# Second layer of a two-layer trunk: the four groups of heads are taken in the order second, first, fourth, third

## The chip, the core and the metric

The kernel runs on one core of a Trainium2 chip. The metric is device time in microseconds (us) of one execution. The engines are TensorE (PE in the profile), VectorE (DVE), ScalarE (ACT), GpSimd (POOL) and SyncE (SP); SP, ACT and POOL each also issue DMA transfers, which all run on the core's 16 DMA engines.

## The reference

The model has two layers over x (1, 512, 2048), float32. The change touches the second one only: an attention layer with forget gates, 16 heads of 128 columns.

```python
h = rms_norm(x, norm_g)
proj = h @ w_in                       # w_in: (2048, 4*2048 + 16), columns [q | k | v | z | forget logits]
q, k, v, z, f_logit = jnp.split(proj, [2048, 4096, 6144, 8192], axis=-1)
q, k = rms_norm(q per head), rms_norm(k per head)
cum = jnp.cumsum(log_sigmoid(f_logit + f_bias), axis=1)          # one row for each head
for each head, block of 128 queries:
    logits = q . k * 128**-0.5 + cum[query] - cum[key];  causal mask;  p = softmax(logits);  out = p @ v
y = out * silu(z)
x = x + y @ w_out                     # w_out: (2048, 2048), 128 rows for each head
```

## The kernel before, in words

Every large product is computed in split precision: an operand is divided into a high and a low part, and three matmuls replace one. For the input projections of both layers a one-level fast scheme (seven block products for eight) is used as well. It needs sums of weight blocks, which VectorE computes, and one sum per step is stored to a scratch tensor (`t2_dram`, printed as `t_rows`) and read back later.

The input projection of the second layer is made in eight *units*, here called units 0 to 7 (`u - UB` in the code). A unit makes 512 columns of q and 512 of k ("qk"), or 512 of v and 512 of z ("vz"), for all 512 positions. Its list of kinds is `KIND`, and `GROUP` says which group of four heads each unit serves: units 0 and 1 serve the first group taken, units 2 and 3 the second, 4 and 5 the third, 6 and 7 the fourth.

A unit has two phases of eight steps. In each step SP loads 128 rows of the weight (or twice 128 in the first phase, 1 MB in all), into one of three buffers `raw`. Each row of such a load is made of two separate pieces of 512 floats (2048 bytes): for "qk" one of q's columns and one of k's. In the second phase SP also reads back the 256 KB sum. The row pitch of the weight is 8208 floats (32,832 bytes), and a group's pieces begin at `c` = 512 columns times the group's number, in each of the four parts q, k, v, z.

Then DVE forms sums in place (L1624, L1626) and the sum to be stored (L1633), ACT makes the high part (`u_hi`, L714), DVE the low part (`u_lo`, L1639), and PE multiplies (L1192 to L1194): 24 matmuls in a step of the first phase, 18 in one of the second; in unit 0 it is the other way round, and its first-phase loads are 768 KB. SP issues the load of step g only when the low part of step g - 3 is made (`lo1_ready`), so the loads run three steps ahead of L1639.

Other work stands between the steps at fixed places. After a "qk" unit that is followed by a "vz" unit, the heads' q and k are normalized and turned (L1403) and stored. Finished v and z are stored too. Unit 2 also makes the forget gates (L1429 to L1431), for all 16 heads at once, and stores their cumulative rows. In the second half of unit 7 POOL and SP load what attention wants first (`qkT`, `vz`, `accb`), and PE begins with the first head. After unit 7 comes the tail: attention of one pair of heads beside the output projection of the pair before, with rows of `w_out` loaded by `load2`.

The order of all this is written out by hand, engine by engine. Scratch tensors hold heads by their position in the order (`qkT_dram`, `vz_dram`); `cum_dram` holds them by their true number.

Of the kernel before, what the change touches and what calls it, by code (L numbers as in the profile page):

```python
# [31 lines left out]
P = 128  # L32
# [3 lines left out]
def build_trunk(nc, x, a_norm_g, a_w_in, a_v_norm_g, a_w_s, a_b_s, a_w_out,  # L36
                b_norm_g, b_w_in, b_f_bias, b_q_norm_g, b_k_norm_g, b_w_out, out):
    SEQ, D = x.shape[1], x.shape[2]
# [6 lines left out]
    HD = b_q_norm_g.shape[1]  # L45
    FB = 512
# [17 lines left out]
    UB = NU  # L64
    KIND = ["qk", "vz", "qk", "vz", "qk", "vz", "vz", "qk"]
    GROUP = [0, 0, 1, 1, 2, 2, 3, 3]
    NB_U = len(KIND)
    NUT = UB + NB_U
    HG = 4
# [17 lines left out]
    cum_dram = nc.dram_tensor("cum_rows", [H, SEQ], F32).ap()  # L87
# [8 lines left out]
    with ExitStack() as ctx:  # L96
        base = (nc.sbuf_base + 31) // 32 * 32

        def at(name, offset, shape, dt=F32):
            return nc.alloc_sbuf_tensor_at(name, shape, dt, offset=base + offset)  # L100
# [60 lines left out]
        cum_row = at("cum_row", 196608, [P, 2, SEQ])  # L161
# [217 lines left out]
        def products_of(u):  # L379

            own = u >= UB and KIND[u - UB] == "vz"
            return [(e1v if own else e1, c11_ready, 0, 1), (cA, c21_ready, 2, 1),
                    (eU, c12_ready, 0, 0), (e57v if own else e57, c22_ready, 2, 0)]
# [3 lines left out]
        def turns_before(u):  # L387

            return 4 * sum(KIND[b] == "vz" and KIND[b - 1] == "qk" for b in range(1, u - UB))

        def stores_before(u):

            return 4 * sum(KIND[b - 1] == "vz" for b in range(1, u - UB))
# [10 lines left out]
        def before(h):  # L404

            return h - 2 if h >= 3 else h - 1 if h == 1 else None

        def side_of(h):
            return 1 if h % 2 or h == 0 else 0

# [10 lines left out]
        def _(sp):  # L421
# [6 lines left out]
            def weights(u, row):  # L428
                if u < VU:
                    return a_v[row:row + P, u, :, :]  # L430
                if u < NU:
                    return a_uz[row:row + P, :, (u - VU) * FB:(u - VU + 1) * FB]
                c = GROUP[u - UB] * FB
                return (b_qk if KIND[u - UB] == "qk" else b_vz)[row:row + P, :, c:c + FB]

            def load_step(u, ph, k):
                g = step_of(u, ph, k)
                slot, loaded = raw_of(g), raw_wait(g)[0]
                if g >= STEPS + 3:
                    sp.wait_ge(lo1_ready, g - 2)  # L440
                elif g >= STEPS:
                    f = g - STEPS
                    sp.wait_ge(x2_stored[f], 16)
                    sp.wait_ge(x_turned, KP + 2 * f + 2)
                    sp.wait_ge(sqb_ready, NT * (f + 1))
                elif g >= 4:
                    sp.wait_ge(lo1_ready, g - 3)
                k1, k2 = weights(u, 2 * k * P), weights(u, (2 * k + 1) * P)
                if ph == 0:
                    sp.dma_start(slot[:, 1:3, :], k1).then_inc(loaded, 16)  # L450
                    if first(u):
                        sp.dma_start(slot[:, 0, :], k2[:, 0, :]).then_inc(loaded, 16)
                    else:
                        sp.dma_start(slot[:, 0:4:3, :], k2).then_inc(loaded, 16)
                else:
                    q = u * KP + k
                    sp.dma_start(slot[:, 0:4:3, :], k2).then_inc(loaded, 16)
                    sp.wait_ge(t2_stored[q % 2], (q // 2 + 1) * 16)
                    sp.dma_start(slot[:, 2, :], t2_dram[k, :, :]).then_inc(loaded, 16)
# [21 lines left out]

            def load2(i):
                p, f, k = i // (2 * NF), i // 2 % NF, i % 2
                row = (2 * p + k) * HD
                if i >= R:
                    sp.wait_ge(lo_ready, B0 + i - R + 1)
                sp.dma_start(w2_raw[:, i % R, :], b_out[row:row + HD, f * FB:(f + 1) * FB])\
                    .then_inc(w_loaded[i % R], 16)
# [22 lines left out]
            for i in range(R, B0):  # L511
                f, k = i // KY, i % KY
# [3 lines left out]
                if f == 0 and 12 <= k < 24:  # L516
                    if k == 12:
                        sp.wait_ge(lo1_ready, STEPS)
                    t, c = (k - 12) % NT, (k - 12) // NT
# [7 lines left out]
            for u in range(UB, NUT):  # L527
                for ph in range(2):
                    for k in range(KP):
                        if step_of(u, ph, k) >= STEPS + 3:  # L530
                            load_step(u, ph, k)
                        if u == NUT - 1 and ph == 1 and k >= 6:
                            for e in range(2):
                                f = 2 * (k - 6) + e
                                sp.wait_ge(step_done, step_of(u, 1, 3 * (k - 6) + 3))
                                sp.dma_start(accb[f][:, :, :], x2_dram[f, :, :, :]).then_inc(accb_loaded[f], 16)
            sp.wait_ge(lo1_ready, STEPS + NB_U * 2 * KP - 2)
            for i in range(2 * NF * NP):
                load2(i)
# [9 lines left out]
        def _(pool):  # L549
# [81 lines left out]
            def store_products(u):  # L631
                g, n = GROUP[u - UB], stores_before(u + 1) // 2
                bufs = products_of(u)
                for i, (buf, _, t0, _) in enumerate((bufs[2], bufs[3])):
                    pool.wait_ge(v_b, n + i + 1)
                    pool.dma_start(vz_dram[0, g, :, t0:t0 + 2, :], buf[:, :, :]).then_inc(vz_stored, 16)
                for i, (buf, _, t0, _) in enumerate((bufs[0], bufs[1])):
                    pool.wait_ge(z_b, n + i + 1)
                    pool.dma_start(vz_dram[1, g, :, t0:t0 + 2, :], buf[:, :, :]).then_inc(vz_stored, 16)

            for u in range(UB + 1, NUT):
# [3 lines left out]
                elif KIND[b] == "vz":  # L645
                    qk_power(turns_before(u) // 4)
                    for r in range(HG):
                        h = turns_before(u) + r
# [5 lines left out]
                    pool.dma_start(cum_dram, cum_T).then_inc(cum_stored, 16)  # L654

            def load_cum(h):
                pool.dma_start(cum_row[:, h % 2, :], cum_dram[h:h + 1, :].broadcast_to([P, SEQ]))\
                    .then_inc(cum_loaded[h % 2], 16)

            def load_qkT(h):  # L660
# [10 lines left out]
            for s in range(2):  # L671
                pool.wait_ge(qkT_stored[s], 16 * (H - HG) // 2)
            load_cum(0)
            load_cum(1)
            pool.wait_ge(step_done, step_of(NUT - 1, 1, 0))
            load_qkT(0)
# [5 lines left out]
            for h in range(H):  # L682
                if h == 3:
                    qk_power(NP // 2 - 1)
                if h + 2 < H:
                    pool.wait_ge(last_logits, h + 1)
                    load_cum(h + 2)
                if h + HG < H - HG:
                    pool.wait_ge(last_scores, h + 1)
                    load_qkT(h + HG)  # L690
                if h % 2 and h // 2 + 2 < NP:
                    pool.wait_ge(yb_ready, h + 1)
                    load_vz(h // 2 + 2)
# [3 lines left out]
        def _(act):  # L697
# [359 lines left out]
            def exps(h):  # L1057
                s = side_of(h)
                for n, i in enumerate(Q_ROWS[0:3]):
                    p = probs[:, s, row_at[i]:row_at[i] + (i + 1) * P]  # L1060
                    act.wait_ge(logits, 3 * h + n + 1)
                    act.activation(p, p, ACT.Exp, scale=-1.0, bias=nmin[:, s, i:i + 1],
                                   accum_out=rsum[:, s, i:i + 1]).then_inc(probs_ready, 1)

            def last_exp(h):
                s = side_of(h)
                p = probs[:, s, row_at[1]:row_at[1] + 2 * P]
                act.wait_ge(last_logits, h + 1)
                act.activation(p, p, ACT.Exp, scale=-1.0, bias=nmin[:, s, 1:2],
                               accum_out=rsum[:, s, 1:2]).then_inc(last_probs, 1)  # L1070

            def probs_turned(h):
                one, two = bank_of(h)
                act.wait_ge(probsT_psum, h + 1)
                for b, bank in enumerate((one, two)):
                    ins = act.activation(probs_T[:, side_of(h), b * 4 * P:(b + 1) * 4 * P], bank, ACT.Copy)
                ins.then_inc(probsT_ready, 1)
# [1108 lines left out]
```

## Time and profile before

| | us |
|---|---|
| median of 3 runs | 2398.81 (2394.89 to 2402.56) |
| profiled execution, its own time | 2398.87 |
| its span in the trace | 2397.0 |
| PE busy | 2290.7 |
| DVE busy | 1616.3 |
| ACT busy | 1065.4 |

The second layer's projection lies between about 1385 and 2100 us of the span. An engine's busy time is the sum over its instructions; what lies between the instructions is idle time, which the view of waits assigns to the engine or the DMA that ended it. The time that the DMA engines took for a queue's packets is given as a share of 16 engines over the stretch that was asked for.

### The profile page before, as it was taken

Reading aid. Unit: us, or ns where it says so; the run is one execution under the profiler, and the core shown is the slowest. Engines: PE = TensorE matmul, PEld = TensorE weight load, DVE = VectorE, ACT = ScalarE, POOL = GpSimd, SP = SyncE. Lnnn points to the kernel's source line nnn. Section 1 sums busy time; section 2 is a strip of 40 time slices with the busy share of each in tenths; the row PEclk is TensorE's granted clock in tenths of the full one; section 3 lists DMA queues with packets and bytes.
Section 4 is the critical chain, followed back from the end, with each engine's and each line's share of the span. In section 5 each row is a group of like instructions: output and inputs, shape, how many; then the busy total and the mean of one; then the engine's idle time right before and its main releaser. Section 6 shows DMA issues by size and latency. Waiting matters only on the chain.

```text
span 2397.0 us, 26493 instructions
## 1 busy us (share of the span) xinstructions
PE 2290.7 (96%) x10413; PEld 1864.1 (78%) x10413; DVE 1616.3 (67%) x1676; ACT 1065.4 (44%) x1319; POOL 134.1 (6%) x185
## 2 busy tenths in 40 slices
PE   5999999999999999999999989999989999989999
PEld 4777787788888878878888877777767777778887
DVE  6787778777877877753222477776766777566665
ACT  6555445454544544552222544343443344344332
POOL 0011011000000000000000000100100000102000
PEclk9999999999999999999999999999999999999999
DMA  6577787776776767765344568885698897845333
GB/s 207 171 248 248 239 260 247 226 236 220 236 227 219 235 218 239 232 226 164 97 115 115 122 160 165 197 271 161 197 226 197 188 279 231 293 137 163 101 96 116
DMA packets 230252, 474.86 MB, mean 198 GB/s; under 512 B 19600, under 2 KB 23744, under 8 KB 229104
## 3 DMA queue, kind: packets, MB, share of 16 engines
q1 hardware_dynamic: 188416, 363.91, 54.2%
q0 software_dynamic: 18576, 67.28, 8.0%
q10 hardware_dynamic: 23136, 41.98, 4.7%
q8 instruction: 82, 1.34, 0.2%
q14 instruction: 42, 0.34, 0.0%
HBM read 391.28 MB, written 81.82 MB: 197 GB/s over the span
## 4 chain that ended last, share of the span: by engine, by line
PE 72%; DVE 11%; DMA 10%; ACT 3%; issue 2%; SPq 0%; POOL 0%; ACTq 0%; DVEq 0%
PE ps L1192 15%; PE ps L1194 15%; PE ps L1193 15%; DVE u_lo L1639 5%; PE ps L1349 4%; PE ps L1351 4%; PE ps L1350 4%; DMA raw<-in_b_w_in_dram 3%; DMA t_rows<-t 3%; DMA raw<-t_rows 3%; PE ps L1572 2%; PE ps L1574 2%; PE ps L1573 2%; DVE raw L1624 2%; ACT u_hi L714 2%
## 5 line engine op out<-in xcount | busy, mean ns | idle before, releaser
L714 ACT ACTIVATE u_hi<-raw 128x1536 fp32r<-128x1536 f32 (+1 forms) x320 | 544.7, 1702 | 822.7 <-PE ps L1194 788.1
L1639 DVE TENSOR_TENSOR u_lo<-raw,u_hi 128x1536 fp32r<-128x1536 f32 (+1 forms) x320 | 646.9, 2022 | 234.7 <-ACT u_hi L714 234.4
L1192 PE MATMUL ps<-u_hi,x1h 128*128 128x512 f32 x1280 | 515.9, 403 | 69.2 <-DVE u_lo L1639 58.7
L1193 PE MATMUL ps<-u_lo,x1h 128*128 128x512 f32 x1280 | 505.2, 395 | 0.0
L1194 PE MATMUL ps<-u_hi,x1l 128*128 128x512 f32 x1280 | 504.4, 394 | 0.0
L1192 PE MATMUL ps<-u_hi,x2h 128*128 128x512 f32 x960 | 381.0, 397 | 5.9 <-DVE u_lo L1639 5.8
L1194 PE MATMUL ps<-u_hi,x2l 128*128 128x512 f32 x960 | 375.1, 391 | 0.0
L1193 PE MATMUL ps<-u_lo,x2h 128*128 128x512 f32 x960 | 374.9, 391 | 0.0
L1192 PEld LDWEIGHTS ps<-u_hi,x1h 128*128 128x128 f32 x1280 | 243.8, 190 | 153.2 <-DVE u_lo L1639 85.4
L1194 PEld LDWEIGHTS ps<-u_hi,x1l 128*128 128x128 f32 x1280 | 244.1, 191 | 53.0
L1193 PEld LDWEIGHTS ps<-u_lo,x1h 128*128 128x128 f32 x1280 | 244.2, 191 | 48.2
L1624 DVE TENSOR_TENSOR raw<-raw 128x1024 f32<-128x1024 f32 x160 | 194.9, 1218 | 65.1 <-DMA raw<-in_b_w_in_dram 65.0
L1835 DVE TENSOR_TENSOR w_lo<-w_raw,w_hi 128x512 fp32r<-128x512 f32 x128 | 88.2, 691 | 210.3 <-ACT w_hi L922 210.3
L1192 PEld LDWEIGHTS ps<-u_hi,x2h 128*128 128x128 f32 x960 | 181.0, 189 | 45.1 <-DVE u_lo L1639 8.3
L1194 PEld LDWEIGHTS ps<-u_hi,x2l 128*128 128x128 f32 x960 | 180.9, 188 | 38.1
L1193 PEld LDWEIGHTS ps<-u_lo,x2h 128*128 128x128 f32 x960 | 181.2, 189 | 36.6
L1349 PE MATMUL ps<-w_hi,yhl 128*128 128x512 f32 x448 | 175.5, 392 | 0.0
L1351 PE MATMUL ps<-w_hi,yhl 128*128 128x512 f32 x448 | 174.4, 389 | 0.0
L1350 PE MATMUL ps<-w_lo,yhl 128*128 128x512 f32 x448 | 174.3, 389 | 0.0
L922 ACT ACTIVATE w_hi<-w_raw 128x512 fp32r<-128x512 f32 x128 | 80.4, 630 | 208.1 <-PE ps L1351 206.1
L1626 DVE TENSOR_TENSOR raw<-raw 128x512 f32<-128x512 f32 x160 | 111.5, 697 | 51.8 <-DMA raw<-t_rows 51.7
L1633 DVE TENSOR_TENSOR t<-raw 128x512 f32<-128x512 f32 x160 | 109.7, 686 | 47.8 <-DMA t_rows<-t 47.2
(232 smaller groups left out, 2418.5 us busy)
## 6 DMA issues: line engine op xcount, KB each, us to landing
raw<-in_a_w_in_dram SPq DMA_DIRECT2D x280, 512.0 KB, 4.4
raw<-in_b_w_in_dram SPq DMA_DIRECT2D x184, 512.0 KB, 5.5
t_rows<-t ACTq DMA_DIRECT2D x160, 256.0 KB, 4.9
raw<-t_rows SPq DMA_DIRECT2D x160, 256.0 KB, 5.1
w_raw<-in_a_w_out_dram SPq DMA_DIRECT2D x128, 256.0 KB, 2.9
w_raw<-in_b_w_out_dram SPq DMA_DIRECT2D x64, 256.0 KB, 2.7
vz<-vz_rows POOLq DMA_DIRECT2D x16, 512.0 KB, 5.4
t<-yT_rows SPq DMA_DIRECT2D x28, 256.0 KB, 3.8
```

What stands on the lines that cost most here:

```text
L714: act.activation(u_hi[:, u_of(g), 0:n, :], raw_of(g)[:, 0:n, :], ACT.Copy).then_inc(hi1_ready, 1)
L1192: pe.matmul(dst[:, t, :], a, u_hi[:, s, pos, :], start=first, stop=False, skip_group_check=more)
L1193: pe.matmul(dst[:, t, :], a, u_lo[:, s, pos, :], start=False, stop=False, skip_group_check=more)
L1194: mm = pe.matmul(dst[:, t, :], b, u_hi[:, s, pos, :], start=False, stop=last, skip_group_check=more)
L1349: pe.matmul(ps[S][:, t, :], a, w_hi[:, s, :], start=start, stop=False)
L1350: pe.matmul(ps[S][:, t, :], a, w_lo[:, s, :], start=False, stop=False)
L1351: mm = pe.matmul(ps[S][:, t, :], b, w_hi[:, s, :], start=False, stop=stop)
L1624: dve.tensor_tensor(m[:, 0:2, :], m[:, 0:2, :], m[:, 1:3, :], ALU.add).then_inc(t_ready, 1)
L1626: dve.tensor_tensor(m[:, 1, :], m[:, 3, :], m[:, 2, :], ALU.add).then_inc(t_ready, 1)
L1633: dve.tensor_tensor(t2[:, q % 2, :], raw_of(g)[:, 0, :], raw_of(g)[:, 2, :], ALU.add)\
L1639: dve.tensor_tensor(u_lo[:, u_of(g), 0:n, :], raw_of(g)[:, 0:n, :], u_hi[:, u_of(g), 0:n, :].bitcast(F32), ALU.subtract).then_inc(lo1_read ...
L1835: dve.tensor_tensor(w_lo[:, i % R, :], w_raw[:, i % R, :], w_hi[:, i % R, :].bitcast(F32), ALU.subtract).then_inc(lo_ready, 1)
```

## The change

A list `GROUP_COLS = [1, 0, 3, 2]` maps the position in the order to the true group of heads. It enters at three places: the columns of `w_in` that a unit loads, the rows of `w_out` that a pair of heads loads, and the row of `cum_dram` that a head loads. The scratch tensors stay indexed by position. The number, order, shapes and waits of the instructions are the same on all engines; only the addresses in HBM of these three kinds of loads differ.

```diff
     GROUP = [0, 0, 1, 1, 2, 2, 3, 3]
+    GROUP_COLS = [1, 0, 3, 2]
...
+        def head_of(h):
+
+            return GROUP_COLS[h // HG] * HG + h % HG
+
...
-                c = GROUP[u - UB] * FB
+                c = GROUP_COLS[GROUP[u - UB]] * FB
                 return (b_qk if KIND[u - UB] == "qk" else b_vz)[row:row + P, :, c:c + FB]
...
-                row = (2 * p + k) * HD
+                row = head_of(2 * p + k) * HD
...
-                pool.dma_start(cum_row[:, h % 2, :], cum_dram[h:h + 1, :].broadcast_to([P, SEQ]))\
+                pool.dma_start(cum_row[:, h % 2, :], cum_dram[head_of(h):head_of(h) + 1, :].broadcast_to([P, SEQ]))\
```

## Rows read from the trace of the kernel before

**Rows 1.** The page, part 1: busy time, share of the span, instructions.

```profile
PE 2290.7 (96%) x10413; PEld 1864.1 (78%) x10413; DVE 1616.3 (67%) x1676; ACT 1065.4 (44%) x1319; POOL 134.1 (6%) x185
```

**Rows 2.** The line L450: duration ns min/median/max, first and last start.

```profile
L450 SPq DMA_DIRECT2D raw<-in_b_w_in_dram x64: 367/368/1372, 1350.6 to 2039.4; - x64
```

**Rows 3.** Timeline of SP's queue where units 2, 4, 6 begin loading.

```profile
1553.64 0.37 SPq L450 DMA_DIRECT2D raw<-in_b_w_in_dram  x1
...
1734.68 0.37 SPq L450 DMA_DIRECT2D raw<-in_b_w_in_dram  x1
...
1919.36 0.37 SPq L450 DMA_DIRECT2D raw<-in_b_w_in_dram  x1
```

**Rows 4.** DMA queues, 1350 to 1551.9 us: packets, MB, share of 16 engines.

```profile
q1 hardware_dynamic: 15079, 28.59, 69.8%
```

**Rows 5.** DMA queues, 1551.9 to 1732.9 us.

```profile
q1 hardware_dynamic: 15469, 29.59, 57.1%
```

**Rows 6.** DMA queues, 1732.9 to 1917.6 us.

```profile
q1 hardware_dynamic: 15351, 29.35, 80.2%
```

**Rows 7.** DMA queues, 1917.6 to 2088.8 us.

```profile
q1 hardware_dynamic: 15504, 31.07, 62.9%
```

**Rows 8.** The tile raw, from 1380 us on: duration min/median/max, first and last start.

```profile
L1639 DVE TENSOR_TENSOR u_lo<-raw,u_hi x128: 1747/2016/2342, 1384.6 to 2099.9; 128x1536 fp32r<-128x1536 f32 x64, 128x2048 fp32r<-128x2048 f32 x64
```

**Rows 9.** Windows, one for each unit's loads (units 0 to 7).

```profile
core 0: us, PE busy (x) PEld busy (x) DVE busy (x) ACT busy (x) POOL busy (x), PEclk, DMA share, GB/s
1384.60:1460.80 76.20, 69.91 (x296) 55.93 (x296) 57.03 (x55) 36.25 (x40) 2.02 (x2) 0.96 0.74 170
1460.80:1551.90 91.10, 84.53 (x365) 68.03 (x364) 70.19 (x63) 36.64 (x29) 5.43 (x1) 0.98 0.88 181
1551.90:1636.60 84.70, 81.76 (x376) 65.96 (x375) 60.30 (x50) 39.79 (x37) 5.50 (x9) 1.00 0.85 254
1636.60:1732.90 96.30, 92.31 (x455) 73.84 (x453) 69.69 (x65) 39.59 (x34) 6.88 (x2) 1.00 0.59 173
1732.90:1827.20 94.30, 82.92 (x366) 65.65 (x365) 59.51 (x48) 40.93 (x36) 4.33 (x8) 1.00 0.94 222
1827.20:1917.60 90.40, 81.83 (x343) 65.03 (x342) 66.58 (x61) 35.65 (x28) 5.46 (x1) 0.96 0.91 187
1917.60:2000.20 82.60, 80.74 (x364) 65.73 (x363) 59.31 (x49) 39.17 (x35) 4.32 (x8) 1.00 0.85 255
2000.20:2088.80 88.60, 82.31 (x354) 65.30 (x353) 60.80 (x57) 37.47 (x36) 9.45 (x16) 0.98 0.88 286
```

**Rows 10.** Waits, 1732.9 to 1827.2 us (unit 4): us in total, times, longest.

```profile
DVE raw L1624 <- DMA raw<-in_b_w_in_dram: 21.1, 8, 4.6
PE ps L1192 <- DVE u_lo L1639: 11.0, 8, 2.9
```

**Rows 11.** Waits, 1917.6 to 2000.2 us (unit 6).

```profile
DVE raw L1624 <- DMA raw<-in_b_w_in_dram: 7.3, 4, 3.5
PE ps L1192 <- DVE u_lo L1639: 1.6, 2, 0.9
```

**Rows 12.** Waits, 1384.6 to 1460.8 us (unit 0).

```profile
PE ps L1192 <- DVE u_lo L1639: 6.3, 4, 3.0
```

**Rows 13.** Waits, 1460.8 to 1551.9 us (unit 1).

```profile
PE ps L1192 <- DVE u_lo L1639: 6.1, 3, 3.0
```

**Rows 14.** Waits, 1827.2 to 1917.6 us (unit 5).

```profile
PE ps L1192 <- DVE u_lo L1639: 8.1, 4, 3.6
```

**Rows 15.** Windows, the first-phase part of units 2, 4, 6; columns as in rows 9.

```profile
1551.90:1597.90 46.00, 43.73 (x201) 35.05 (x200) 33.29 (x27) 24.69 (x25) 3.78 (x7) 1.00 0.89 282
...
1732.90:1788.00 55.10, 45.97 (x207) 36.01 (x205) 33.48 (x26) 26.11 (x26) 3.80 (x7) 1.00 1.00 230
...
1917.60:1963.30 45.70, 43.84 (x202) 35.23 (x201) 33.46 (x28) 24.45 (x25) 3.78 (x7) 1.00 0.91 277
```

**Rows 16.** DMA queues and issues, 2000.2 to 2088.8 us (unit 7); issues end in us to landing.

```profile
q0 software_dynamic: 1888, 6.82, 20.2%
...
vz<-vz_rows POOLq DMA_DIRECT2D x4, 512.0 KB, 9.4
```

**Rows 17.** Window, the tail; columns as in rows 9.

```profile
2088.80:2397.00 308.20, 297.61 (x1585) 242.68 (x1583) 193.46 (x381) 115.60 (x267) 25.33 (x33) 0.99 0.38 125
```

## The prediction

> **What bounds the kernel now.** I read the page first. PE is busy 96% of the span [rows 1], so the end is set by PE and by whatever makes it wait. The change alters only HBM addresses, so the one thing that can move is how long some loads take. I therefore looked for places where PE waits behind loads, and whether loads of different groups take different times.
>
> The first load of the second layer's projection is issued at 1350.6 us [rows 2]. The loads of the second, third and fourth group begin at 1553.64, 1734.68 and 1919.36 [rows 3]. I cut the trace close to these places and asked each stretch for SP's queue (q1). Its engine time per packet is share x 16 x stretch / packets:
> - group 0: 0.698 x 16 x 201.9 / 15079 = 149.5 ns [rows 4]
> - group 1: 0.571 x 16 x 181.0 / 15469 = 106.9 ns [rows 5]
> - group 2: 0.802 x 16 x 184.7 / 15351 = 154.4 ns [rows 6]
> - group 3: 0.629 x 16 x 171.2 / 15504 = 111.1 ns [rows 7]
>
> That is the reading on which everything rests. Packet counts and bytes are nearly equal (28.6 to 31.1 MB), the kinds of unit are the same, yet the columns of groups 0 and 2 take 40% more engine time than those of groups 1 and 3, and it switches twice back and forth where the group switches. I call them slow and fast groups. Why the address does this, no row says.
>
> Then by unit. The 128 instructions of L1639 [rows 8] are the steps in order. Loads run three steps ahead, so I cut unit n's stretch from its step -3 to its step 13 [rows 9]; unit 0 starts at step 0. Units 4 and 6 are the clean pair: both follow a "vz" unit, with the same stores and the same extra work of DVE and PE. Unit 4 (slow) takes 94.3 us at a DMA share of 0.94, unit 6 (fast) 82.6 at 0.85: 11.7 us apart. The engines' time is 0.94 x 94.3 = 88.6 against 0.85 x 82.6 = 70.2 us, 18.4 us more for slow columns. In unit 4 DVE waits 21.1 us for the weights and PE 11.0 us for DVE [rows 10]; in unit 6 it is 7.3 and 1.6 [rows 11]. The difference is nearly all in the first phase, which asks 1 MB of each step: 55.1 us in unit 4 (DMA share 1.00), 46.0 and 45.7 in units 2 and 6 [rows 15].
>
> **The change part by part.** The columns of w_in: today positions 0 to 3 in the order (units 0-1, 2-3, 4-5, 6-7) are slow, fast, slow, fast. Afterwards they are fast, slow, fast, slow. The slow traffic is not less; it stands beside other work. So units 0, 1, 4, 5 gain, and units 2, 3, 6, 7 lose.
>
> Gains:
> - Unit 4 becomes what unit 6 is: 94.3 - 82.6 = 11.7 us.
> - Unit 5 waits 8.1 us at PE [rows 14] where a fast unit waits 1.6; that is 6.5. Against unit 6's length it would be 90.4 - 82.6 = 7.8. PE has the same number of turned heads in both stretches, but DVE is busier (66.6 against 59.3 us). I take 7.
> - Unit 1: 6.1 - 1.6 = 4.5 [rows 13], or 91.1 - 82.6 = 8.5. I take 7, since it does unit 5's work.
> - Unit 0: 6.3 - 1.6 = 4.7 [rows 12]; its first phase loads only three quarters. Its granted clock is 0.96 of full speed, with the drops to the lower level behind PE's waits; up to 0.04 x 76.2 = 3.0 more if they go. Bounds 0 and 7.7, I take 5, close to the row.
>
> Sum 30.7, bounds 22.7 to 35.7.
>
> Losses:
> - Unit 6 becomes what unit 4 is: 11.7.
> - Unit 7 has no slow model. By its engines' time: 0.88 x 88.6 = 78.0, plus 18.4 is 96.4 us. At unit 4's share of 0.94 that needs 102.5 us (+13.9), at a share of 1.00 still 96.4 (+7.8). It carries attention's first loads as well, 20.2% of the engines on POOL's queue, its vz loads landing after 9.4 us [rows 16]. Between the ends I take 11.
> - Unit 2: its first phase has 46.0 us, like unit 6's 45.7, and would become unit 4's 55.1: +9.1. By engine time (0.85 x 84.7 + 18.4) / 0.94 = 96.2, +11.5. Its second phase begins the forget gates' matmuls, under which loads catch up; the lower bound is 0. I take 9.
> - Unit 3 has room: its share is 0.59 of 96.3 us, because the gates' work holds PE. 0.59 x 96.3 + 18.4 = 75.2 us fits well. Only the first phase's later steps can be short of data. Bounds 0 and 5 (half of unit 2's 9.1, for half of the steps), I take 2.
>
> Sum 33.7, bounds 19.5 to 42.1.
>
> The rows of w_out and of the cumulative sums: the tail is 308.2 us with PE busy 297.6 and a DMA share of 0.38 [rows 17]. Packets that took 40% longer would still be hidden; if that cover were gone, PE's whole gap there is 10.6 us. A permutation of equal row blocks adds nothing: 0. The order in which DVE, ACT and PE work is untouched: 0.
>
> Total: -30.7 + 33.7 = +3.0 us on the profiled execution's 2398.87, which lies 0.06 above the median, so 2402. The outermost ends are -35.7 + 19.5 = -16 and -22.7 + 42.1 = +19. A time within 0.3% of the one before, 7.2 us, is what a measurement here can't tell from no change.
>
> **A rule beside the row.** The packets of slow and fast groups are alike in size, and the trace has 150 ns against 107 to 111 for them [rows 4 to 7]. The Trainium skill (page "DMA: Bandwidth & Descriptors", section "Specifications") gives a transfer size from which the line rate is reached, 512 bytes, and ties no rate to the address; by it pieces of 2048 bytes cost the same in all groups, and the change would be worth nothing. The trace disagrees with that. It is the first rival below.
>
> **The rivals.**
> - *The addresses do not matter*: the four stretches would be slow and fast for a reason tied to time, not to columns. For it: nothing in the program explains why. Against it: the same kinds of units in the same places fall on both sides, and the changes coincide with the group's first load three times. Time: 2399, no change. Chance 0.12.
> - *The DMA engines fill up* (slower): where a slow unit meets stores and attention's loads, the length follows the engine time at a share of 0.94. That makes unit 2 +11.5, unit 7 +13.9 and unit 3 +5: 11.7 + 13.9 + 11.5 + 5 = 42.1 against gains of 30.7, +11.4, so 2410. For it: unit 4 runs at that share [rows 9]. Against: what is left of the stretch behind the first-phase part is alike in the fast unit 2 (84.7 - 46.0 = 38.7 us) and the slow unit 4 (94.3 - 55.1 = 39.2), so only first phases pay [rows 9, 15]. It decides once the losses pass 30.7 + 7.2 = 37.9. Chance 0.32.
> - *The forget gates hide the second group* (faster): PE's extra work in units 2 and 3 lets the slow loads of both catch up, so that they cost 0 in place of 11. Then 30.7 - 22.7 = -8.0, 2391. For it: unit 3's share of 0.59. Against: that work comes after unit 2's first phase, which is already at 0.89 [rows 15]. It decides when units 2 and 3 together cost less than 0.8 us, or a few us with the gains at their upper end. Chance 0.20.
>
> **How the numbers follow.** The forecast, the two halves nearly cancel, has 0.36. Within 0.3%: 0.36 + 0.12 = 0.48; slower 0.32, faster 0.20. The range reaches from just past the hidden-gates case, 2390, to beyond the full-engines case with its terms at the upper end, 2416.
>
> **What would show it.** In the new profile q1's time per packet should be near 110, 150, 110, 155 ns in the four stretches. Unit 4 should be near 83 us and unit 6 near 94, unit 2 near 94, and unit 7 near 100, and PE's waits for L1639 should move with them. I am wrong if the pattern stays in time (first rival), or if one of units 2 and 7 is far from its term; unit 7 is the least certain one, since no slow row carries its mix.

## The result

The change made the kernel slower by 0.6%: 2411.11 us against 2397.42 (medians of 9 runs each), ratio 1.006 with a 95% interval of 1.0043 to 1.0076. Its single times spread from 2397.75 to 2422.24 us, those of before from 2394.68 to 2402.56. The profiled execution is the fastest of the nine, 2397.75 us, so its trace shows the mechanism well and the size badly.

In the page of the changed kernel PE's part is as before [rows 1]:

```profile
span 2395.9 us, 26493 instructions
...
PE 2286.1 (95%) x10413; PEld 1861.3 (78%) x10413; DVE 1617.1 (67%) x1676; ACT 1065.5 (44%) x1319; POOL 137.4 (6%) x185
```

The DMA queues of the changed kernel, in the stretches of its four groups (1350 to 1538.1, to 1733.1, to 1897.8, to 2089.3 us); columns as in [rows 4 to 7]:

```profile
q1 hardware_dynamic: 14556, 27.61, 51.3%
...
q1 hardware_dynamic: 15385, 29.42, 72.9%
...
q1 hardware_dynamic: 15381, 29.41, 62.3%
...
q1 hardware_dynamic: 15430, 30.49, 75.9%
```

By the same division as in the prediction that is 106, 148, 107 and 151 ns a packet, where before it was 150, 107, 154 and 111. The slow stretches have moved with the columns.

The windows of the changed kernel, one for each unit's loads, cut at the same steps and with the same columns as [rows 9]:

```profile
1379.60:1452.40 72.80, 68.15 (x296) 54.93 (x296) 56.91 (x56) 36.32 (x40) 2.01 (x2) 0.98 0.61 181
1452.40:1538.10 85.70, 82.35 (x363) 66.90 (x362) 70.09 (x62) 36.64 (x29) 6.34 (x1) 1.00 0.65 192
1538.10:1632.20 94.10, 84.37 (x377) 66.84 (x377) 60.35 (x50) 39.85 (x37) 5.51 (x9) 0.98 0.94 226
1632.20:1733.10 100.90, 94.12 (x456) 74.97 (x454) 70.09 (x65) 39.59 (x33) 7.00 (x2) 0.98 0.77 167
1733.10:1815.20 82.10, 80.98 (x365) 65.99 (x364) 59.58 (x49) 40.83 (x36) 4.34 (x8) 1.00 0.84 257
1815.20:1897.80 82.60, 77.99 (x342) 62.72 (x341) 66.60 (x60) 35.20 (x28) 6.37 (x1) 1.00 0.69 203
1897.80:1991.70 93.90, 85.85 (x366) 69.19 (x365) 59.44 (x47) 39.38 (x35) 4.33 (x8) 0.95 0.94 224
1991.70:2089.30 97.60, 83.40 (x353) 64.94 (x352) 60.88 (x57) 37.51 (x36) 9.47 (x16) 0.98 0.99 254
```

Against [rows 9], units 0, 1, 4 and 5 are shorter by 3.4, 5.4, 12.2 and 7.8 us (28.8 in all), units 2, 3, 6 and 7 longer by 9.4, 4.6, 11.3 and 9.0 (34.3). The sum of the eight goes from 704.2 to 709.7, +5.5 us. That this execution still ends 1.1 us earlier comes from elsewhere: 5.0 us up to the first step of unit 0 (1379.6 against 1384.6), and 1.6 in the tail (306.6 against 308.2). The changed columns are not what moves that first step: over the profiles of all kernels here it lies between 1378.3 and 1386.3 us where unit 0 has fast columns, and between 1380.9 and 1389.2 where it has slow ones.

The waits have moved along. In the changed kernel, unit 2 (1538.1 to 1632.2 us) looks like [rows 10] now:

```profile
DVE raw L1629 <- DMA raw<-in_b_w_in_dram: 19.8, 7, 4.2
...
PE ps L1197 <- DVE u_lo L1644: 9.7, 7, 3.0
```

All lines are 5 further down than in the kernel before. In unit 4 (1733.1 to 1815.2 us) PE waits less than in [rows 11]:

```profile
PE ps L1197 <- DVE u_lo L1644: 0.9, 1, 0.9
```

### The profile page after: what moved, and what is told of

Same layout as the page of the kernel before. It is cut to its first block, busy times and chain, and to the rows that moved or that the text cites. A ratio compares the mean times of both kernels' runs of the same rounds, so it can differ in the third digit from the quotient of the medians.

```text
span 2395.9 us, 26493 instructions
## 1 busy us (share of the span) xinstructions
PE 2286.1 (95%) x10413; PEld 1861.3 (78%) x10413; DVE 1617.1 (67%) x1676; ACT 1065.5 (44%) x1319; POOL 137.4 (6%) x185
## 4 chain that ended last, share of the span: by engine, by line
PE 73%; DVE 11%; DMA 10%; ACT 3%; issue 2%; POOL 1%; SPq 0%; ACTq 0%; DVEq 0%
PE ps L1197 15%; PE ps L1199 14%; PE ps L1198 14%; DMA raw<-in_b_w_in_dram 5%; DVE u_lo L1644 5%; PE ps L1356 5%; PE ps L1355 5%; PE ps L1354 5%; PE ps L1577 2%; PE ps L1579 2%; PE ps L1578 2%; DMA raw<-t_rows 2%; DMA t_rows<-t 2%; ACT u_hi L719 2%; DVE raw L1629 2%
## 5 line engine op out<-in xcount | busy, mean ns | idle before, releaser
L1638 DVE TENSOR_TENSOR t<-raw 128x512 f32<-128x512 f32 x160 | 109.8, 686 | 40.1 <-DMA t_rows<-t 39.2
```

Source lines behind the costliest of these rows:

```text
L1638: dve.tensor_tensor(t2[:, q % 2, :], raw_of(g)[:, 0, :], raw_of(g)[:, 2, :], ALU.add)\
```

## The experiments

All times are compared with runs of the kernel before on the same chip. A difference in us to the kernel before is worked out from the ratio; the plain difference of the medians can be up to 2.4 us off it. In each kernel's trace the 128 steps were counted and the units cut as above.

**The changed kernel again.** The only edit is a comment.

> The changed kernel once more, for a second profile. Its timed runs spread over 24 us where the profiled one has 2398. Theory: the slow columns cost more in some executions, so a longer execution shows longer units 2, 3, 6, 7 (together over 387 us, their sum in the first profile of the changed kernel). Rival: the extra lies elsewhere (first layer or tail), then these four keep their sum within 3 us.

It took 2415.74 us (one run), with a span of 2413.8, 17.9 over that of the first profile. Its windows for units 2, 3, 6 and 7:

```profile
1544.40:1640.70 96.30, 85.26 (x376) 67.78 (x375) 60.40 (x50) 39.81 (x37) 5.51 (x9) 0.96 0.95 220
1640.70:1741.90 101.20, 94.05 (x456) 75.01 (x454) 69.95 (x64) 39.65 (x34) 6.88 (x2) 0.98 0.78 166
...
1907.00:2004.60 97.60, 86.65 (x366) 69.35 (x365) 59.34 (x48) 39.44 (x35) 4.33 (x8) 0.95 0.91 215
2004.60:2105.90 101.30, 85.96 (x354) 67.42 (x353) 60.94 (x56) 37.71 (x36) 9.47 (x16) 0.95 0.98 245
```

Their sum is 396.4 us against 386.5, +9.9. Of the other 8.0 us, 5.7 lie ahead of unit 0, 1.3 in the tail and 1.0 in the remaining units. So the theory holds and the rival has a part: more than half of the difference between the two executions is in the slow units, and a third lies ahead of unit 0, where other kernels here vary as much.

**The columns alone, and the rows alone.**

```diff
 columns only:
-                c = GROUP[u - UB] * FB
+                c = [1, 0, 3, 2][GROUP[u - UB]] * FB
 rows only (from the changed kernel):
-                c = GROUP_COLS[GROUP[u - UB]] * FB
+                c = GROUP[u - UB] * FB
```

> Only the columns of the input projection are permuted; the rows of the output projection and of the cumulative sums are as before, so heads meet other heads' rows. Theory: this is the whole change, 6 to 14 us slower than before (2403 to 2411). Rival (the output rows matter): nearer 2397.

> Only the rows of the output projection and of the cumulative sums are permuted, the columns are as before. Theory: no change, 2397 within 3 us. Rival (the output rows matter in the tail): 3 us or more.

The columns alone gave 2415.84 us, ratio 1.0058 (1.0038 to 1.0078): as much as the whole change (1.006). The rows alone gave 2397.03, ratio 0.999 (0.9976 to 1.0005): nothing that can be measured. The tail of the kernel with the rows alone is no longer than that of the kernel before [rows 17], and as little loaded:

```profile
2098.10:2402.20 304.10, 294.57 (x1585) 240.95 (x1583) 193.59 (x381) 115.61 (x267) 25.32 (x33) 1.00 0.39 125
```

These two kernels also give a third profile of the changed columns and a second one of the old columns. The units' sum is 709.7, 720.6 and 726.1 us with the changed columns (mean 718.8) and 704.2 and 708.9 with the old ones (mean 706.6). The difference is 12.2 us, close to the 13.7 between the medians. The whole spans of these five differ by only 8.4 us in the mean, because with the changed columns the first step of unit 0 happened to come 4.7 us earlier. The agreement of the sums with the medians is thus partly chance.

The kernel with the columns alone shows where a slow unit can grow. The windows of its unit 2, the first-phase part and the rest:

```profile
1544.60:1601.60 57.00, 49.48 (x212) 39.43 (x212) 33.43 (x26) 24.76 (x25) 3.79 (x7) 0.94 0.99 222
1601.60:1647.60 46.00, 39.39 (x166) 31.03 (x165) 26.75 (x25) 14.95 (x12) 1.72 (x2) 0.93 0.79 186
```

In the changed kernel's first profile they were these:

```profile
1538.10:1593.10 55.00, 47.17 (x207) 37.39 (x207) 33.45 (x27) 24.75 (x25) 3.79 (x7) 0.97 0.99 233
1593.10:1632.20 39.10, 37.20 (x171) 29.45 (x170) 26.91 (x25) 15.10 (x12) 1.72 (x2) 1.00 0.87 216
```

The rest took 46.0 us in one and 39.1 in the other. In the long one the chain that ended last (start us, us, what) runs through a stored sum and its reading back:

```profile
1596.85 10.32 DMA t_rows<-t
...
1612.87 12.01 DMA raw<-t_rows
```

In the long one a store of 256 KB that was issued at the end of the saturated first phase took 10.3 us and a read of 256 KB 12.0; over the whole kernel before, the medians of such transfers are 4.9 and 5.1. In the short one the chain has a read that began at 1595.81 us and took 9.24, and no store, so the late store is what the two differ in most. PE's waits for the low part in that stretch, long one first:

```profile
PE ps L1192 <- DVE u_lo L1639: 6.6, 3, 2.8
...
PE ps L1197 <- DVE u_lo L1644: 1.9, 3, 0.8
```

That is 4.7 of the 6.9 us. The other 2.2 are PE's busy time (39.39 against 37.20, for five matmul records fewer): its mean granted clock was 0.93 of full speed, between its two levels of 1.2 and 2.4 GHz, where it was 1.00 in the short one, and a matmul on the chain took 0.43 us for a while and not 0.23. So this stall costs twice: the wait, and matmuls at the lower level after it.

The other traces bear this out. A unit 2 or 4 (both qk) with wholly slow columns and uncut loads stands eleven times in the profiles. The four longest (103.0, 101.1, 99.8 and 99.6 us) all have such a store of 9.7 to 10.5 us on their chain and a mean granted clock of 0.92 or 0.93. The five of 93.3 to 96.3 us have none on it, at 0.96 to 1.00. Between them lie 98.8 us without such a store, at 0.97, and 97.9 with one, at 0.98. What makes a store come late in one execution and not in another, no run here shows.

**Other orders.**

```diff
 slow last:
-    GROUP_COLS = [1, 0, 3, 2]
+    GROUP_COLS = [1, 3, 0, 2]
 slow first:
-    GROUP_COLS = [1, 0, 3, 2]
+    GROUP_COLS = [0, 2, 1, 3]
```

> Order second, fourth, first, third: the slow columns in units 4 to 7. Theory (cost by place, from the two profiles: units 0-1 about 9 us, 2-3 about 14, 4-5 about 20, 6-7 about 20): 12 us over the kernel before, 2409. q1 per packet near 107, 111, 150, 154 ns in the four stretches. Rival (slowness goes with time, not columns): 2397 and the old pattern of packet times.

> Order first, third, second, fourth: the slow columns in units 0 to 3. Theory: their cost there is 9 + 14 = 23 us against 29 in the kernel before, so 6 us faster, 2391. Rival (the slow traffic costs the same wherever it stands): 2397.

Slow last: 2414.77 us, ratio 1.0052 (1.0026 to 1.0078), 12.5 us over the kernel before; packet times 106, 106, 154, 152 ns. Slow first: 2394.83, ratio 0.9977 (0.9961 to 0.9992), 5.5 us under it; 149, 152, 107, 108 ns. Both came out as expected. The place matters, and the first four units together bear the slow columns best. They do not hide them: units 2 and 3 of slow first are

```profile
1546.90:1648.00 101.10, 89.82 (x378) 71.32 (x377) 60.42 (x52) 40.06 (x37) 5.51 (x9) 0.92 0.93 211
1648.00:1748.60 100.60, 94.02 (x455) 74.94 (x454) 70.01 (x65) 39.60 (x33) 6.88 (x2) 0.98 0.78 167
```

against 84.7 and 96.3 in [rows 9]. What units 4 and 5 gain there (19.6 us) is no more than what units 2 and 3 lose (20.7); the eight units sum to 703.2 us against 704.2 and 708.9 in the two profiles of the old columns. The 5.5 us rest on the timed runs, and these profiles do not show where they come from.

**Only fast, only slow columns.**

```diff
-                c = GROUP[u - UB] * FB
+                c = [1, 3, 1, 3][GROUP[u - UB]] * FB      # all odd;  all even: [0, 2, 0, 2]
```

> All units load columns of the second and fourth group (each twice; the first and third are left out). Theory: no slow stretch, 29 us under the kernel before, about 2368; all packets near 107 to 111 ns. Rival (time, not columns): 2397.

> All units load columns of the first and third group (each twice; the others are left out). Theory: all stretches slow, 34 us over the kernel before, about 2431, packets near 150 ns everywhere. Rival (time, not columns): 2397.

All odd: 2368.44 us, ratio 0.9876 (0.9849 to 0.9902), 30 us under the kernel before, with 106 ns in all four stretches. All even: 2437.71 us, ratio 1.0164 (1.0135 to 1.0194), 39 us over it, with 146, 152, 156, 152 ns. The slow columns cost 30 us in the kernel before and could cost 69. The sums of the eight units, 676.0 and 739.3 us, say nearly the same. Unit by unit, slow columns cost 25.9 us in units 0 to 3 and 37.4 in units 4 to 7. With this the rival that the slow stretches belong to the time and not to the columns is gone.

**Other starts.**

```diff
-                c = GROUP[u - UB] * FB
+                c = [256, 768, 1280, 128][GROUP[u - UB]]
```

> The four pairs of units load 512 columns that begin at 256, 768, 1280 and 128 (other columns than the reference's), to see how the packet time goes with the start. Theory that parity of the 512-column block decides: 256 and 1280 half slow (about 130 ns), as 768 would be; 128 nearer to slow. Rival: only starts at even blocks are slow, and all four stretches are near 110 ns.

Its queues in the four stretches (1350 to 1541.9, to 1738.9, to 1904.9, to 2102.3 us), for the starts 256, 768, 1280 and 128:

```profile
q1 hardware_dynamic: 15058, 28.55, 52.2%
...
q1 hardware_dynamic: 15373, 29.39, 74.9%
...
q1 hardware_dynamic: 15403, 29.45, 60.7%
...
q1 hardware_dynamic: 15468, 30.93, 68.0%
```

That is 106, 154, 105 and 139 ns; the one run took 2408.77 us. Neither expectation held: 256 and 1280 are wholly fast, 768 wholly slow, 128 between. With the groups' own starts (0 and 1024 slow, 512 and 1536 fast) the pattern repeats every 1024 columns, 4096 bytes, as far as it was tried; within one period 768 and 0 are slow, 128 in part, 256 and 512 fast. These are positions within a row. The rows are 32,832 bytes apart, which is 8 x 4096 + 64, so each row starts 64 bytes further against that period, and the 128 rows of one load pass through it twice. The pieces of a load thus begin at the same set of remainders modulo 4096 for every start that was tried. Only which row has which remainder differs.

**Smaller transfers.** The kernel before, its second-layer loads cut into two or four transfers by partitions.

```diff
+                    w = P // CUT                  # CUT = 2 or 4
+                    def cut(dst, of):
+                        for i in range(CUT):
+                            sp.dma_start(dst[i * w:(i + 1) * w], of[i * w:(i + 1) * w]).then_inc(loaded, 16)
```

> The kernel before, with each load of the second layer's projection issued as two transfers of 64 partitions in place of one of 128: the same rows and columns, but another set of rows is read at the same time by the 16 engines. Theory (the slow columns come from which addresses are read together): the packet times change with the cut, in slow or in fast columns, by over 10 ns. Rival (a column block is slow in itself): q1 stays near 150 and 107 ns in the slow and fast stretches, time 2397 or a little more from more transfers.

> The same with four transfers of 32 partitions. Theory: packet times of the slow columns move again, further from 150 ns; if the slow columns fall to the fast ones' time, up to 26 us faster (2372). Rival: 150 and 107 ns stay, and the additional transfers cost SP's issue time (0.37 us each, up to 8 more than before in a step of about 5.5 us), slower than before.

Halves: 2406.95 us, ratio 1.0049 (1.003 to 1.0068). Quarters: 2411.13, ratio 1.0045 (1.0028 to 1.0062). The packets' number grows with the cut at nearly the same bytes (in group 1's stretch 15469, 16436 and 18475), so the engines' time is the better measure. For halves, in the stretches of group 1 (1551.0 to 1731.1 us) and group 2 (1731.1 to 1917.3):

```profile
q1 hardware_dynamic: 16436, 29.47, 67.0%
...
q1 hardware_dynamic: 16399, 29.39, 81.7%
```

0.670 x 180.1 = 121 us for group 1 against 0.571 x 181.0 = 103 before, and 0.817 x 186.2 = 152 for group 2 against 148. With quarters it is 109 and 151, although their packet times in the slow stretches fall to 128 and 132 ns: there are only more packets. The columns of groups 0 and 2 are not relieved; those of groups 1 and 3 got dearer, most with halves. The expectations are met in the letter (107 to 118 ns with halves, in the fast columns, and both cuts slower, as the rival of the quarters had it), but the test does not separate what is read together from the cost of more transfers. It stays inconclusive, and the cut is no cure.

**A slow and a fast block in one load.**

```diff
-                c = GROUP[u - UB] * FB
-                return (b_qk if KIND[u - UB] == "qk" else b_vz)[row:row + P, :, c:c + FB]
+                g = GROUP[u - UB]
+                of = (b_qk if KIND[u - UB] == "qk" else b_vz)[row:row + P, :, g * FB:(g + 1) * FB]
+                if KIND[u - UB] == "vz":          # all mixed: if True
+                    (s0, n0), (s1, n1), (s2, n2) = of.ap
+                    return bass.AP(of.tensor, of.offset, [[s0, n0], [s1 + ((g ^ 1) - g) * FB, n1], [s2, n2]])
+                return of
...
-                    pool.dma_start(vz_dram[1, g, :, t0:t0 + 2, :], buf[:, :, :]).then_inc(vz_stored, 16)
+                    pool.dma_start(vz_dram[1, g ^ 1, :, t0:t0 + 2, :], buf[:, :, :]).then_inc(vz_stored, 16)
```

> The kernel before, but each vz unit loads v of its own group and z of the neighbour (one slow block and one fast block in every load); z is stored under the neighbour's number, so all is computed as before. Theory: a load's cost grows faster than its packet time, because PE covers a part of it: a mixed unit at about 130 ns costs under half of a slow one. Units 1 and 5 gain about 3 and 4 us, units 3 and 6 lose about 1 and 4: near 0 to 3 us faster, 2397. Rival (cost is proportional, or a block beside another is slow as a whole at 150 ns): no gain, or units 3 and 6 lose 5 and 12 us and the time is 2405 or more.

> The same in the qk units too (q of one group with k of the neighbour, so other scores than the reference's are computed). Theory: all four stretches near 130 ns and no first-phase part of 55 us; the sum of the slow terms, 26 us in the kernel before, falls to about half, 2387. Rival: 150 ns everywhere, 2430 or more.

With the vz units mixed: 2384.2 us, ratio 0.994 (0.9918 to 0.9963), 14 us under the kernel before, which makes it the shortest of the versions here that leave nothing out. All mixed: 2369.36 us, ratio 0.988 (0.9854 to 0.9907), as fast as with fast columns alone. The gains are larger than expected, for a reason that I had not seen. The windows of the kernel with mixed vz units, units 1, 3, 4, 5 and 6:

```profile
1459.30:1545.00 85.70, 82.38 (x363) 66.89 (x363) 70.13 (x63) 36.70 (x29) 6.34 (x1) 1.00 0.63 193
...
1628.20:1724.10 95.90, 92.14 (x454) 73.87 (x453) 69.61 (x64) 39.56 (x33) 6.88 (x2) 1.00 0.56 173
1724.10:1823.70 99.60, 87.02 (x365) 69.71 (x364) 59.39 (x47) 40.83 (x36) 4.33 (x8) 0.93 0.89 211
1823.70:1906.30 82.60, 77.74 (x341) 62.73 (x341) 66.50 (x61) 35.15 (x28) 6.37 (x1) 1.00 0.66 202
1906.30:1988.40 82.10, 80.66 (x365) 66.06 (x364) 59.84 (x47) 39.45 (x35) 4.32 (x8) 1.00 0.81 258
```

Units 1 and 5 are as short as with fast columns (85.7 and 82.6), though half of what they load is a "slow" block; units 3 and 6 lose nothing. Unit 4, a qk unit of group 2 that is not mixed, is slow as ever. All mixed, q1 in the second stretch (1541.7 to 1721.9 us) reads

```profile
q1 hardware_dynamic: 15438, 29.52, 53.1%
```

which is 99 ns a packet, below every unmixed fast stretch. So no block is slow in itself. Slow, as far as these runs go, are transfers whose two pieces lie 8192 bytes apart and begin near a multiple of 4096 bytes within rows of 32,832 bytes; with one of the pieces shifted by 2048 bytes the same columns load fast. "Near" means beginning 1024 bytes below such a multiple (768) or on it (0), in part 512 bytes above it (128), and no longer 1024 above it (256). The two pieces as two transfers of their own were not tried, so whether they must be in one transfer to be slow stays open.

## Why the prediction was right, and where it was off

The measured 2411.11 us lies in the range of 2390 to 2416, but not where the forecast put it: 2402 is 9 us less, and the range reaches that far only because the slower rival was taken into it. The pattern, the signs of all eight units and the gains were right; the losses were too small. By its parts:

- *What bounds, and the reading of packet times*: right. The four stretches have 106, 148, 107 and 151 ns, where I had written 110, 150, 110 and 155, and the kernel with only the columns changed has the whole effect. That the column block is slow in itself, which my words "slow group" imply, was wrong: the mixed loads show that it is the pair of pieces. For this change it made no difference, since both pieces move together.
- *Unit 4 becomes what unit 6 is, and the reverse*: right in the first profile, -12.2 and +11.3 us for 11.7 each. Over the profiles at hand (three with the changed columns, two with the old ones) the means are -14.9 and +12.1.
- *Units 5, 1 and 0*: I took 7, 7 and 5; the means are 7.6, 4.5 and 2.0. Unit 5 fits, though one reason given for it is not so: PE turns 8 blocks in unit 5's stretch and 24 in unit 6's (L1403), 1.4 and 4.0 us, and not the same number. Unit 1 ends at its lower bound: a fast unit 1 takes 85.7 us and not unit 6's 82.6. DVE is busy for 70.1 us of it and no longer waits for the weights (9.4 us before), yet PE still waits 3.3 us for the low part. Unit 0 gains less than I took; why, no run isolates.
- *Unit 7*: 11 taken, 10.8 in the mean. The first profile has a DMA share of 0.99 and 97.6 us there, near the end that I had worked out for a share of 1.00.
- *Unit 2 was mis-sized*: 9 taken, 9.4, 11.6 and 18.3 in the three profiles, against 84.7 (mean 13.5 against the old columns' mean). The step that failed is that what lies behind the first-phase part is alike for slow and fast columns (38.7 in unit 2 and 39.2 in unit 4). The clean pair already spoke against it: in the fast unit 6 that rest is 82.6 - 45.7 = 36.9, 2.3 less than in unit 4. In the changed kernel it was as taken in one profile (39.1 us). In the kernel with the columns alone a stored sum lands late behind the first phase, its reading back is slow, and PE's clock falls as well (46.0 us). One profile of a slow unit 4 could not show this; the second one, with 99.8 us for it, does.
- *Unit 3*: 2 taken, 4.8 measured, at the upper bound. The forget gates' work does not hide the slow loads, so the faster rival is out.
- *The rows of w_out*: nothing, as predicted, with the kernel of the rows alone.

The losses came to 41.2 us in the mean (13.5 + 4.8 + 12.1 + 10.8) where I had 33.7, the gains to 29.0 where I had 30.7. That is +12.2 instead of +3.0. It falls into the slower rival, whose price was 42.1 against 30.7, +11.4 us and 2410. That the sums agree so closely is in part luck. The rival let the length follow the engines' time at a share of 0.94. Unit 2 ran at 0.90 to 0.95 but also paid for the late store, which the rival does not name (13.5 us, its price 11.5). Unit 7 ran at a higher share, 0.98 to 0.99, and cost less (10.8, its price 13.9). Unit 3 cost 4.8 at a share of 0.77 to 0.79, so the engines were not full there. The likeliest case in my list was that the halves cancel, and this was not the case that came.

The Trainium skill's size rule (page "DMA: Bandwidth & Descriptors", section "Specifications") gives 512 bytes as the least transfer for line rate. It does not suffice here: packets of the same 2048-byte pieces took from 105 to 156 ns, by their addresses alone. That no rate is tied to an address can be said of that section only, not of the whole skill.

## What to carry to other kernels

When a change moves only addresses, ask the trace for DMA time per packet in stretches that follow the addresses: loads of equal size need not cost the same. A saturated phase can cost more than its own length, since stores and reads that a later phase needs come late behind it, so a single profile of a lucky execution understates it. If two pieces of a row are read in one transfer, try another distance between them before reordering the work: it took away what the order could only move.

## What the runs showed of the hardware

- The same number of 2048-byte packets took up to 45% more DMA engine time at some column starts of a matrix with rows of 32,832 bytes: 154 ns a packet at column 768, 106 at 256, 139 at 128.
- Pairing each block with its neighbour, so that the pieces lie 6144 or 10,240 bytes apart and not 8192, brought all stretches to 99 to 103 ns. What decides this, no run here shows.
- Cutting the transfers of fast columns in two raised the engines' time for them from 103 to 121 us in a stretch of about 180; in four, to 109.
- Behind a stretch at a DMA share of 0.99, a 256 KB store took 10.3 us and a 256 KB read 12.0, against medians of 4.9 and 5.1 over the kernel before.
